# Rotating the queries of a latent attention: one projection and half tiles in place of a projected, swapped copy

## The reference

```python
q = (rmsnorm(cq, q_norm_g) @ w_uq).reshape(b, s, MLA_HEADS, MLA_NOPE + MLA_ROPE)
q_nope, q_rope = q[..., :MLA_NOPE], q[..., MLA_NOPE:]
...
q_rope = rope(q_rope, positions)
k_rope = rope(k_rope[:, :, None, :], positions)
q_mla = jnp.concatenate([q_nope, q_rope], axis=-1)
k_mla = jnp.concatenate(
    [k_nope, jnp.broadcast_to(k_rope, (b, s, MLA_HEADS, MLA_ROPE))], axis=-1)
...
def rope(x, positions):
    ...
    x1, x2 = xf[..., : r // 2], xf[..., r // 2:]
    out = jnp.concatenate([x1 * cos - x2 * sin, x2 * cos + x1 * sin], axis=-1)
```

## Time and profile before

| what | us |
| --- | --- |
| median of 3 runs (lowest to highest) | 1002.73 (1002.03 to 1002.77) |
| the profiled execution: its own time | 1001.97 |
| its span, first to last instruction | 999.9 |
| busy in the span: TensorE, VectorE, ScalarE | 991.0, 719.4, 597.8 |
| granted TensorE clock, mean | 0.999 |

### The profile page before, as it was taken

One profiled execution on the slowest core, in us unless ns is written; L12 is line 12 of the kernel. 1 busy time (PEld: TensorE's weight loads), 2 busy tenths in 40 slices (PEclk: granted clock), 3 DMA queues, 4 the chain that ended last, 5 costly groups with the idle time before them and its releaser, 6 DMA issues.

```text
span 999.9 us, 16659 instructions
## 1 busy us (share of the span) xinstructions
PE 991.0 (99%) x6652; PEld 891.9 (89%) x6652; DVE 719.4 (72%) x1225; ACT 597.8 (60%) x1010; POOL 0.4 (0%) x5
## 2 busy tenths in 40 slices
PE   9999999999999999999999999999999999999997
PEld 8899999998888888999999888888999899888886
DVE  5898888878888888887658665655776558565652
ACT  4778665557566657767647445554665547455452
POOL 0000000000000000000000000000000000000000
PEclk9999999999999999999999999999999999999999
DMA  9975667535556664563326655555554327555521
GB/s 367 404 251 183 261 231 288 201 137 211 209 195 234 221 238 166 211 211 127 127 85 217 210 205 198 182 177 206 214 187 144 127 106 253 194 186 176 205 82 42
DMA packets 28443, 196.72 MB, mean 197 GB/s; under 512 B 3152, under 2 KB 3664, under 8 KB 5584
## 3 DMA queue, kind: packets, MB, share of 16 engines
q1 hardware_dynamic: 28224, 195.41, 54.6%
q10 hardware_dynamic: 144, 0.26, 0.1%
HBM read 194.61 MB, written 1.05 MB: 196 GB/s over the span
## 4 chain that ended last, share of the span: by engine, by line
PE 95%; DMA 1%; DVE 1%; ACT 1%; issue 1%; SPq 0%; DVEq 0%; ACTq 0%
PE PS L1382 16%; PE PS L1269 10%; PE PS L1069 8%; PE PS L1252 8%; PE PS L1070 7%; PE PS L1071 7%; PE PS L1273 5%; PE PS L1255 4%; PE PS L1222 3%; PE PS L1225 3%; PE PS L1223 3%; PE PS L1361 2%; PE PS L1363 2%; PE PS L1362 2%; PE PS L1303 2%; PE PS L1304 2%
## 5 line engine op out<-in xcount | busy, mean ns | idle before, releaser
L1948 DVE TENSOR_TENSOR wlo<-raw,whi 128x1024 fp32r<-128x1024 f32 x306 | 358.4, 1217 | 61.0 <-ACT whi L1544 58.3
L1544 ACT ACTIVATE whi<-raw 128x1024 fp32r<-128x1024 f32 x300 | 297.8, 1047 | 58.7 <-PE PS L1382 53.1
L1069 PE MATMUL PS<-HX,whi 128*128 128x256 f32 x496 | 145.1, 293 | 0.9 <-ACT GA L1735 0.5
L1070 PE MATMUL PS<-HX,whi 128*128 128x256 f32 x496 | 140.2, 283 | 0.0
L1071 PE MATMUL PS<-HX,wlo 128*128 128x256 f32 x496 | 140.1, 282 | 0.0
L1269 PE MATMUL PS<-HX,whi 128*128 128x512 f32 x416 | 130.4, 395 | 0.0
L1252 PE MATMUL PS<-HX,whi 128*128 128x512 f32 x320 | 113.3, 398 | 0.0
L1069 PEld LDWEIGHTS PS<-HX,whi 128*128 128x128 f32 x496 | 94.8, 191 | 6.6 <-issue 4.3
L1070 PEld LDWEIGHTS PS<-HX,whi 128*128 128x128 f32 x496 | 95.0, 191 | 0.2
L1071 PEld LDWEIGHTS PS<-HX,wlo 128*128 128x128 f32 x496 | 94.9, 191 | 0.0
L1273 PEld LDWEIGHTS PS<-HX,wlo 128*128 128x128 f32 x416 | 78.1, 188 | 18.2
(11 more groups left out here) (280 smaller groups left out, 2016.8 us busy)
## 6 DMA issues: line engine op xcount, KB each, us to landing
raw<-wall SPq DMA_DIRECT2D x151, 1024.0 KB, 5.0
raw<-wada SPq DMA_DIRECT2D x18, 1024.0 KB, 5.0
raw<-wall SPq DMA_DIRECT2D x8, 512.0 KB, 16.8
GA<-wada SPq DMA_DIRECT2D x2, 1024.0 KB, 21.6
GA<-alibi SPq DMA_DIRECT2D x1, 2048.0 KB, 9.4
raw<-wall SPq DMA_DIRECT2D x2, 768.0 KB, 5.8
X<-xt SPq DMA_DIRECT2D x1, 1024.0 KB, 5.1
KM<-wada SPq DMA_DIRECT2D x1, 1024.0 KB, 14.3
```

Source lines behind the costliest of these rows:

```text
L1069: e.matmul(dst, wh, a, start=start, stop=False, skip_group_check=share)
L1070: e.matmul(dst, wh, b, start=False, stop=False, skip_group_check=share)
L1544: e.activation(whi[place(n)][:, c], raw[i % RAW][:, c], ACT.Copy).then_inc(*up("a_whi", (n, half)))
L1948: e.tensor_tensor(wlo[place(n)][:, c], raw[i % RAW][:, c], f32(whi[place(n)][:, c]), ALU.subtract).then_inc(*up("v_wlo", (n, half)))
```

## The change

The swapped copy of the rotated features is no longer projected. The second `uq` chunk now has 256 columns instead of 512: the first halves (16 features) of all 8 heads in one output tile of 128, the second halves in another. One pair of tiles is projected; VectorE multiplies both tiles with the cosines and with the sines, and takes a difference for the first halves and a sum for the second ones. The chunk is loaded and split at half its size (`USED`, `HALF`), by pieces of 512 and 256 columns.

In `TT` a head's 16 first features now stand beside another head's in groups of 32 rows. `copy_rope` therefore copies each group of 32 rows for a pair of heads, first halves to rows 64 to 95 of `QM` and second halves to rows 96 to 127, in two chores of four copies. The key tile has, for even heads, zeros where the odd head's features stand, and the other way round: `turn_key` makes 64 rows, and `copy_key` writes them in two operations with a scale per partition (columns `even` and `odd` in place of `sgn`). The scores of the MLA heads now contract over 128 rows instead of 96. The step `signs` is gone.

```diff
--- before.py
+++ after.py
@@ -41,7 +41,7 @@
     for name, n in [
         ("c", 8), ("b_ada", 48), ("norm_mix_g", 8), ("norm_ffn_g", 8), ("norm_final_g", 8),
         ("q_norm_g", 3), ("kv_norm_g", 2), ("conv_w", 132), ("conv_b", 44), ("attn_norm", 16),
-        ("mlp_norm", 16), ("subln", 1), ("b_forget", 1), ("invf", 1), ("sgn", 1),
+        ("mlp_norm", 16), ("subln", 1), ("b_forget", 1), ("invf", 1), ("even", 1), ("odd", 1),
         ("eps", 1), ("m1", 8), ("m2", 8), ("m3", 1), ("m4", 1), ("id", 128),
     ]:
         COLS[name] = at
...
@@ -75,7 +75,10 @@
     return order
 
 
-USED = {"uq": 1536}
+USED = {("uq", 0): 1536, ("uq", 1): 768}
+
+
+HALF = {("uq", 1): 512}
 
 
 def stream_order():
...
@@ -362,7 +365,6 @@
             next_tile(7, lambda: emit("slice", s, parts[2:5]), lambda: emit("slice", s, parts[5:7]))
             st["have"] = 3
             taken(3)
-            emit("signs")
             emit("root_table")
             emit("slice", s, parts[7:])
             ensure(4)
...
@@ -403,14 +405,13 @@
     rows(("in", 6), "mix", evac=lambda n, b, pr: emit("ev_heads", n, b, pr, "QF", 4))
 
     def ev_uq_rope(n, b, pr):
-        emit("ev_uq_rope", n, b, pr)
-        if pr == 1:
-            chores.append(lambda: emit("copy_rope"))
+        emit("ev_uq_rope", n, b)
+        chores.extend([lambda: emit("copy_rope", 0), lambda: emit("copy_rope", 1)])
 
     rows(("uq", 0), "lat", pairs=2, mid=False, evac=lambda n, b, pr: emit("ev_queries", n, b, pr))
     heads["all"].append(("fox", 0))
     tokens(("in", 7), "mix", lambda n, b: emit("ev_vf", n, b, 0))
-    rows(("uq", 1), "lat", pairs=2, mid=False, evac=ev_uq_rope)
+    rows(("uq", 1), "lat", mid=False, evac=ev_uq_rope)
     heads["all"].append(("fox", 1))
     tokens(("in", 8), "mix", lambda n, b: emit("ev_vf", n, b, 1), fill=False)
     n = NUMBER[("ukv", 0)]
...
@@ -976,7 +977,11 @@
         return 4 + i // 2 + 2 * (i % 2)
 
     def half_cols(n, half):
-        return slice(half * CH // 2, min(USED.get(ORDER[n][0], CH), (half + 1) * CH // 2))
+        cut = HALF.get(ORDER[n], CH // 2)
+        return slice(half * cut, min(USED.get(ORDER[n], CH), (half + 1) * cut))
+
+    def half_with(n, last):
+        return (last - 1) // HALF.get(ORDER[n], CH // 2)
 
     STEPS = stages()
     marks = Marks(nc, ctx)
...
@@ -1229,6 +1234,8 @@
             elif step == "rows":
                 n, src, b, pr, nt = a
                 hi, lo, kts, ncols, x0 = features(n, src)
+                if ORDER[n] == ("uq", 1):
+                    ncols = 256
                 slot = place(n)
                 if nt == 0:
                     bank(b)
...
@@ -1455,9 +1462,9 @@
                         on.wait_ge("v_f" if i // 2 else "a_f", ("queries", 4 * (i // 2)))
                     elif kind == "mla":
                         h = 2 * i + j
-                        q, k = QM[0:96, h, :], KM[0:96, h, :]
+                        q, k = QM[:, h, :], KM[:, h, :]
                         on.wait_ge("v_ev", (NUMBER[("uq", 0)], 1))
-                        on.wait_ge("a_qr", 0)
+                        on.wait_ge("a_qr", 1)
                         on.wait_ge("a_kr", 0)
                         on.wait_ge("a_ev", (NUMBER[("ukv", 0)], 1))
                     else:
...
@@ -1709,14 +1716,19 @@
                     *up("a_f", "keys"))
             elif step == "copy_key":
                 on.wait_ge("v_kr", "turned")
-                e.activation(
-                    KM[64:96, :, :], V[64:96, 0, 256:512].unsqueeze(1).to_broadcast([32, 8, T]), ACT.Copy).then_inc(
-                    *up("a_kr", 0))
+                for h0, mask in ((0, "even"), (1, "odd")):
+                    m = e.activation(
+                        KM[64:128, h0:8:2, :], V[64:128, 0, 256:512].unsqueeze(1).to_broadcast([64, 4, T]), ACT.Identity,
+                        scale=col(mask, 0, 1, 64, 128))
+                m.then_inc(*up("a_kr", 0))
             elif step == "copy_rope":
+                i, = a
                 on.wait_ge("v_qr", "sum")
                 for j in range(4):
-                    m = e.activation(QM[64:96, j:8:4, :], TT[32 * j:32 * j + 32, :, :], ACT.Copy)
-                m.then_inc(*up("a_qr", 0))
+                    m = e.activation(
+                        QM[64 + 32 * i:96 + 32 * i, 2 * j:2 * j + 2, :],
+                        TT[32 * j:32 * j + 32, i, :].unsqueeze(1).to_broadcast([32, 2, T]), ACT.Copy)
+                m.then_inc(*up("a_qr", i))
                 sq_free[0] = sq_free[1] = ("v_qr", "sum")
             elif step == "ev_vf":
                 n, b, j = a
...
@@ -1926,8 +1938,7 @@
             e.reciprocal(dst, dst).then_inc(*up("v_rec", name))
 
         def trig_there():
-            on.wait_ge("a_sin", 0)
-            on.wait_ge("v_rope", "signs")
+            on.wait_ge("a_sin", 1)
 
         for step, *a in STEPS:
             if step == "weights":
...
@@ -2049,9 +2060,6 @@
                     e.tensor_scalar(rc, rc, math.pi / 2, None, ALU.add).then_inc(*up("v_rope", "c6"))
                     on.wait_ge("v_rope", "c6")
                     e.tensor_scalar(rc, rc, 3.1415925, -3.1415925, ALU.min, ALU.max).then_inc(*up("v_rope", "cosine"))
-            elif step == "signs":
-                on.wait_ge("a_sin", 1)
-                e.tensor_scalar(SIN[:, :], SIN[:, :], col("sgn"), None, ALU.mult).then_inc(*up("v_rope", "signs"))
             elif step == "final_gain":
                 on.wait_ge("d_small", 0)
                 e.tensor_tensor(GC[:, :], col("norm_final_g", 0, 8), col("attn_norm", 0, 8), ALU.mult)
...
@@ -2201,26 +2209,27 @@
                 e.tensor_copy(QM[0:64, 4 * pr:4 * pr + 4:2, :], two(b)[0:64])
                 e.tensor_copy(QM[0:64, 4 * pr + 1:4 * pr + 4:2, :], two(b)[64:128]).then_inc(*up("v_ev", (n, pr)))
             elif step == "turn_key":
-                k0, k1 = V[64:96, 0, 256:512], V[64:96, 1, 256:512]
+                k0, k1 = V[64:128, 0, 256:512], V[:, 1, 256:512]
                 on.wait_ge("a_ev", (FIRST, 1))
                 trig_there()
-                e.tensor_tensor(k0, FK[64:96, :], COS[64:96, :], ALU.mult)
-                e.tensor_tensor(k1, FK[96:128, :], SIN[96:128, :], ALU.mult).then_inc(*up("v_kr", "parts"))
+                e.tensor_tensor(k0, FK[64:128, :], COS[64:128, :], ALU.mult)
+                e.scalar_tensor_tensor(k1[64:96], FK[96:128, :], -1.0, SIN[96:128, :], ALU.mult, ALU.mult)
+                e.tensor_tensor(k1[96:128], FK[64:96, :], SIN[64:96, :], ALU.mult).then_inc(*up("v_kr", "parts"))
                 on.wait_ge("v_kr", "parts")
-                e.tensor_tensor(k0, k0, k1, ALU.add).then_inc(*up("v_kr", "turned"))
+                e.tensor_tensor(k0, k0, k1[64:128], ALU.add).then_inc(*up("v_kr", "turned"))
             elif step == "ev_uq_rope":
-                n, b, pr = a
-                dst, table = ((TT[:, :, :], COS), (SQ[:, 0:2, :], SIN))[pr]
-                on.wait_ge("t_mm", (n, pr))
+                n, b = a
+                on.wait_ge("t_mm", (n, 0))
                 trig_there()
                 is_free(tt_free, 0, 1)
                 on.wait_ge("t_sq", "kv")
-                e.tensor_tensor(dst, two(b), table[:, :].unsqueeze(1).to_broadcast([128, 2, T]), ALU.mult).then_inc(
-                    *up("v_qr", pr))
-                if pr == 1:
-                    on.wait_ge("v_qr", 1)
-                    e.tensor_tensor(TT[:, :, :], TT[:, :, :], SQ[:, 0:2, :], ALU.add).then_inc(*up("v_qr", "sum"))
-                    tt_free[0] = tt_free[1] = ("a_qr", 0)
+                cosines, sines = (x[:, :].unsqueeze(1).to_broadcast([128, 2, T]) for x in (COS, SIN))
+                e.tensor_tensor(TT[:, :, :], two(b), cosines, ALU.mult)
+                e.tensor_tensor(SQ[:, 0:2, :], two(b), sines, ALU.mult).then_inc(*up("v_qr", "parts"))
+                on.wait_ge("v_qr", "parts")
+                e.tensor_tensor(TT[:, 0, :], TT[:, 0, :], SQ[:, 1, :], ALU.subtract)
+                e.tensor_tensor(TT[:, 1, :], TT[:, 1, :], SQ[:, 0, :], ALU.add).then_inc(*up("v_qr", "sum"))
+                tt_free[0] = tt_free[1] = ("a_qr", 1)
             elif step == "gated":
                 n, i, b0, b1 = a
                 gm, gf = pair(GA, 2 * i), pair(GA, 8 + 2 * i)
...
@@ -2467,9 +2476,9 @@
     r = np.arange
     cut = np.cumsum([0, 384, 256, 32, 512, 512, 512, 8, 1024, 1024])
     cq, ckv, kr, fq, fk, fv, ff, gm, gf = (r(cut[i], cut[i + 1]) for i in range(9))
-    sw = np.concatenate([r(16, 32), r(16)])
-    cols_in = np.concatenate([cq, np.tile(ff, 8), kr, kr[sw], ckv, fk, fq, fv, gm, gf])
-    uq = np.concatenate([p + 96 * h for p in (r(64), 64 + r(32), 64 + sw) for h in range(8)])
+    kr1, kr2 = kr[0:16], kr[16:32]
+    cols_in = np.concatenate([cq, np.tile(ff, 8), kr1, kr1, kr2, kr2, ckv, fk, fq, fv, gm, gf])
+    uq = np.concatenate([p + 96 * h for p in (r(64), 64 + r(16), 80 + r(16)) for h in range(8)])
     ukv = np.concatenate([np.concatenate([r(64) + 128 * h for h in range(8)]),
```

(13 more changed lines are left out.)

## The result

The changed kernel takes 1005.26 us (median of 8 runs, 1004.91 to 1005.94) against 1002.34 for the kernel before, measured beside it (8 runs): a ratio of 1.0030, interval 1.0021 to 1.0039, so 2.9 us slower where 1.97 were forecast. Its profiled execution took 1005.41 us, with a span of 1003.6.

What follows compares the result with a forecast made beforehand. VectorE and ScalarE were taken to set the pace up to 150.95, TensorE from there. 2.55 us for the second copies less 0.58 won earlier gave +1.97 on the median 1002.73: 1004.7, range 1001.9 to 1005.6.

Steps and rivals of the forecast that it cites:

- likeliest case: VectorE and ScalarE's chain moves by +1.0 to +2.4 us: 1003.7 to 1005.1, forecast 1004.7, chance 0.70.
- three signs of being wrong: Last gate copy no later than now, TensorE's waits below 1 us, or the granted clock leaving 1.00.
- TensorE's saving: Second `uq` chunk: 18 of 36 matmuls go, 2.16 us less, all spent waiting; as a deciding rival 1000.6, chance 0.05.
- The lead that is left at the turn: At the turn of 108.79, which needs VectorE's scaling, TensorE's lead shrinks to about 0.6 us.
- VectorE ahead of the rotation: Cast and low half take 1.6 us, 1.2 less; with `signs` and `turn_key`, about 1.0 earlier at the first score pass.
- ScalarE ahead of the rotation: `copy_key` in two operations takes 2.17 us, 0.26 more; first head's exponentials start at 79.5, 0.65 earlier.
- The lead of 0.58 us at the first set: ScalarE's first set of `copy_rope` copies starts about 0.58 us earlier than 87.95.
- The second set: Four more copies on ScalarE between the high halves of chunks 13 and 14: 2.55 us, bounds 2.0 and 2.6.
- Undiminished to the gate copy: From chunk 14's low half VectorE and ScalarE have no slack, so the gate copy comes the full 1.97 us later.
- The granted clock at 1.00: TensorE's granted clock stays at 1.00; leaving it would show the prediction wrong.
- among the rivals: Clock falls behind TensorE's stall at 114 us, halving its pace: 1005.4 to 1008.6, say 1007, chance 0.10.
- Waits at two places: TensorE waits for gate copies 2.5 us at 114.0 to 116.5 and 0.5 us later, plus once for VectorE's scaling.

Runs made afterwards that it cites:

- after_warm10: Changed kernel plus 10 matmuls of ones in front of the third gate chunk, run inside TensorE's wait for the gate copy: 1004.59 us, ratio 1.0022.
- after_apart: Changed kernel with only the first half of each of the two late modulation sums moved to a score PSUM bank: 1003.56 us, ratio 1.0009.
- later: Changed kernel with the second set of `copy_rope` copies two refills later, behind chunk 17's high half on ScalarE: 1001.48 us, ratio 0.9993.
- before_twice: Kernel before with the `copy_rope` set issued a second time, where the changed kernel has its second set, into rows nothing reads: 1005.88 us, ratio 1.0033.

## Why the prediction was right, and where it was not

The sign and the mechanism hold, and 1005.26 lies in the range of 1001.9 to 1005.6; the likeliest case's own range, up to 1005.1, it misses by 0.2. That it lies in the range is in part luck: the forecast stood on a median of 1002.73 for the kernel before, which came out at 1002.34 beside the changed one, and 2.92 on the former would be 1005.65. One of the prediction's three signs of being wrong also came true: the granted clock left 1.00. Two terms make the 0.95 us between the forecast's +1.97 and the +2.92.

- *TensorE's saving, 2.16 us:* right in size. The changed chunk's 18 matmuls start from 79.15 and the next group at 81.31, so 18 take 2.16 us. Right too that it is spent waiting. The lead that is left at the turn was given as 0.6; the prediction's own 108.4 would leave 0.4, and 0.70 were measured (108.74, less 0.65, against 108.79): the turn starts behind the first of the four scalings, which run from 108.40, and not behind the last.
- *VectorE ahead of the rotation:* right. Cast and low half go from 71.01 to 72.59, 1.58 us; 1.6 was worked out.
- *ScalarE ahead of the rotation:* right. `copy_key` takes 2.19, worked out as 2.17, and the exponentials begin as the table load ends, at 80.19; less the 0.65 us of the late start that is 79.54, against 79.5.
- *The lead of 0.58 us at the first set:* right. 88.04 against 87.95 is 0.09 later, less 0.65: 0.56 earlier.
- *The second set, 2.55 us:* mis-sized, by 0.3. From the first set to chunk 14's high half the delay grows from 0.09 to 2.93 us (101.92 against 98.99), so it cost 2.84. The four copies take their 2.55, but their neighbours lose the overlaps that they had among themselves. Before, two pieces of a high half took 1.90 us to the next instruction's start (96.61 to 98.51); here 2.02 (96.70 to 98.72). From the values copy to the high half it was 0.48 us, and is 0.63. I had counted the overlaps that the new instructions might win, between 2.0 and 2.6, and none that they break. The Trainium skill's page "ScalarE: Activation LUTs", section "What ACT_TABLE_LOAD costs", has neighbours overlap by some 93 ns. The rows of before agree between whole-tile copies, with 0.10 and 0.11 us (96.61 and 2.00 against 98.51, 98.51 and 0.59 against 98.99); on either side of the 32-row copies the changed kernel shows no overlap but gaps of 0.02 and 0.03. The prediction's 100.04 is the end of the first of the two pieces of chunk 14's high half, for which VectorE waited, and not of the whole, which ended at 100.99.
- *Undiminished to the gate copy:* right. 116.88 against 113.96 is 2.92 later, as much as at chunk 14. Less the late start, 2.27; that alone gives 1004.6, which `after_warm10` measured as 1004.59.
- *The granted clock at 1.00:* wrong. The clock fell at 119, and this added some 0.7 us. It was among the rivals, at 0.10, with a price (for a stretch as long as the wait) of 1.25 us less 0.5, that is 0.75. It came to about that because two errors cancel: the stretch was 3.3 us and not 2.5, and cost 1.5, and the wait that it replaced was worth 0.75 and not 0.5. The stall of 2.5 us was itself forecast; that it would cost the clock was what I gave too little weight. The Trainium skill's page "TensorE: Matmul & The Clock Gate", section "Why this matters for your kernels", warns against idle gaps between bursts of matmuls, but only against longer ones than this. The measurement decides: in this trace the gap of 2.5 us at 115 was followed by 0.50 at 119.
- *Waits at two places, 2.5 and 0.5 us:* the first to the tenth (from 114.32 to 116.86 with the late start taken off, where 114.0 to 116.5 was forecast), and the 0.8 at the turn; the second was swallowed by the slow stretch, and the 0.46 at the values copy was not seen.

So the ledger is 0.56 us won ahead of the rotation, 2.84 lost at the second set, 0.67 lost to the clock: 2.95 against 2.92 measured.

What stays open is what parts the two groups of times of `after_apart`, and why the clock fell 1.4 us after the restart in one kernel and 0.5 in the other.

## What to carry to other kernels

An instruction's price is set by its place on its queue: the same four copies cost 2.84 us ahead of a weight split that two engines wait for, and no time that shows two refills later, where the engine stood idle anyway. Work taken from an engine that is 99% busy pays only if that engine is nowhere held by the others; here the set moved back, a freed bank and a copy moved ahead were needed before 2.35 us arrived, and 0.97 of them are the bank's, which the kernel before gains as well. When a forecast has the busiest engine standing still for microseconds, price the clock behind it too.

## What the runs showed of the hardware

TensorE's granted clock kept its level through waits up to 1.1 us (`later`, `after_apart`, `after_warm10`) and fell to half behind both of the waits of 2.5 us (the changed kernel and `before_twice`). It fell not during the wait but when work had resumed, 1.4 us behind the first matmul in the one and 0.5 in the other, and stayed down for some 3.3 us of dense matmuls in both. The row of the second:

```profile
118.30:121.60 3.30, 3.30 (x17) 3.30 (x16) 3.19 (x7) 1.31 (x2) 0.00 (x0) 0.50 0.25 102
```

A wait can hold TensorE up by more than its row says: 0.76 us for a row of 0.51 in the kernel before.

The start of a launch is not the same in every execution. Windows of the changed kernel, in which TensorE runs the matmuls of ones that open the program:

```profile
4.00:5.00 1.00, 1.00 (x7) 1.00 (x7) 0.00 (x0) 0.98 (x2) 0.00 (x0) 1.00 1.02 426
5.00:6.00 1.00, 1.00 (x6) 1.00 (x6) 0.00 (x0) 0.00 (x0) 0.00 (x0) 1.00 1.01 418
6.00:7.00 1.00, 1.00 (x10) 1.00 (x9) 0.74 (x2) 0.74 (x2) 0.00 (x0) 1.00 1.01 418
```

They go from 6 or 7 in a microsecond to 10 or more at 6 us, though the granted clock of the rows is 1.00 throughout. In the profile of the kernel before this came at 4 us:

```profile
3.00:4.00 1.00, 1.00 (x7) 1.00 (x6) 0.17 (x1) 0.58 (x2) 0.00 (x0) 1.00 0.89 352
4.00:5.00 1.00, 1.00 (x11) 1.00 (x10) 0.00 (x0) 0.99 (x2) 0.00 (x0) 1.00 0.98 410
```

The first reciprocal of VectorE in the changed kernel's profile came at 12.09 in place of 10.94, and 0.65 us of that were left at 44. Moments of two single executions can't be compared to better than this without a row ahead of the change.
